# Two transformer blocks on one core: the order of work at six seams between stages

## The reference

```python
def first_block(x, c, ...):                      # two layers
    for layer in range(2):
        sh_a, sc_a, gt_a, sh_m, sc_m, gt_m = split(silu(c) @ ada_w[layer] + ada_b[layer])
        h = modulate(rms_norm(x, attn_norm[layer]), sh_a, sc_a)
        mix = diff_attention(h, ...) if layer == 0 else nsa_attention(h, ..., *shared)
        x = x + gt_a * mix
        x = x + gt_m * squared_relu_mlp(modulate(rms_norm(x, mlp_norm[layer]), sh_m, sc_m), ...)
        if layer == 0:                           # keys and values that layer 1 shares
            shared = nsa_shared_kv(modulate(rms_norm(x, kv_norm), ...), w_kv, cmp_pos, cmp_w1, cmp_w2)
    return rms_norm(x, final_norm)

def second_block(h, p, ...):                     # a gated recurrence, then dilated attention
    h = ple_add(h + mlstm_layer(h, ...), p[0], ...)
    k, v = shared_kv(h, ...)                     # k: per-head rms_norm, then rope
    h = h + dilated_layer(h, k, v, ...)          # q: per-head rms_norm, then rope
    return ple_add(h, p[1], ...)
```

## Time and profile before

| | |
|---|---|
| median of 3 runs | 1986.16 us (1981.65 to 1990.62) |
| the profiled execution's own time | 1987.13 us |
| its span, first to last instruction | 1985.3 us |
| mean granted TensorE clock | 0.995 |
| TensorE busy | 1925.7 us, 97% |
| VectorE, ScalarE, GpSimd busy | 1168.0, 855.1, 4.8 us |
| chain that ended last, by engine | TensorE 89%, VectorE 6%, ScalarE 2% |

### The profile page before, as it was taken

One profiled execution on the slowest core, in us unless ns is written; L12 is line 12 of the kernel. 1 busy time (PEld: TensorE's weight loads), 2 busy tenths in 40 slices (PEclk: granted clock), 3 DMA queues, 4 the chain that ended last, 5 costly groups with the idle time before them and its releaser, 6 DMA issues.

```text
span 1985.3 us, 24671 instructions
## 1 busy us (share of the span) xinstructions
PE 1925.7 (97%) x9444; PEld 1592.9 (80%) x9444; DVE 1168.0 (59%) x2063; ACT 855.1 (43%) x1370; POOL 4.8 (0%) x5
## 2 busy tenths in 40 slices
PE   5999999999999999999999999999999999999999
PEld 3876778888887887889888888888877888787987
DVE  7657776565657476767464343336753554766564
ACT  3246633232233543657433222234444534667453
POOL 0000000000000000000000000000000000000000
PEclk9999999999999999999899999999999999999999
DMA  9831155555544331000123232222221231241021
GB/s 358 317 150 43 49 199 209 202 184 196 199 181 148 106 108 62 1 1 1 55 85 106 85 106 86 104 92 98 85 85 64 83 136 64 85 149 64 1 96 64
DMA packets 42377, 223.87 MB, mean 113 GB/s; under 512 B 4476, under 2 KB 5244, under 8 KB 23854
## 3 DMA queue, kind: packets, MB, share of 16 engines
q1 hardware_dynamic: 41906, 222.37, 30.9%
q10 hardware_dynamic: 380, 0.28, 0.1%
HBM read 219.45 MB, written 3.19 MB: 112 GB/s over the span
## 4 chain that ended last, share of the span: by engine, by line
PE 89%; DVE 6%; ACT 2%; issue 1%; DMA 1%; SPq 0%; DVEq 0%; ACTq 0%
PE bank L434 24%; PE bank L436 24%; PE bank L435 24%; PE bank L1748 3%; PE bank L1718 2%; PE bank L3021 1%; PE bank L1707 1%; PE bank L798 1%; PE bank L2355 1%; PE bank L540 1%; PE bank L1709 1%; PE bank L818 1%; PE bank L442 1%; DMA x<-x_d 1%; PE bank L2964 1%
## 5 line engine op out<-in xcount | busy, mean ns | idle before, releaser
L434 PE MATMUL bank<-hH,wH 128*128 128x512 f32 x1280 | 501.8, 392 | 3.7 <-DVE hL L580 3.1
L436 PE MATMUL bank<-hH,wL 128*128 128x512 f32 x1280 | 498.3, 389 | 0.0
L435 PE MATMUL bank<-hL,wH 128*128 128x512 f32 x1280 | 498.1, 389 | 0.0
L1080 ACT ACTIVATE wH<-raw 128x2048 fp32r<-128x2048 f32 x64 | 122.7, 1917 | 463.1 <-PE bank L436 463.1
L1125 DVE TENSOR_TENSOR wL<-raw,wH 128x2048 fp32r<-128x2048 f32 x64 | 146.6, 2291 | 268.5 <-ACT wH L1080 268.5
L434 PEld LDWEIGHTS bank<-hH,wH 128*128 128x128 f32 x1280 | 240.3, 188 | 55.3 <-DVE hL L580 3.0
L435 PEld LDWEIGHTS bank<-hL,wH 128*128 128x128 f32 x1280 | 240.3, 188 | 50.4 <-issue 1.0
L436 PEld LDWEIGHTS bank<-hH,wL 128*128 128x128 f32 x1280 | 240.2, 188 | 50.1
L411 DVE TENSOR_TENSOR wL<-raw,wH 128x2048 fp32r<-128x2048 f32 x71 | 162.6, 2289 | 153.4 <-ACT wH L406 153.1
L406 ACT ACTIVATE wH<-raw 128x2048 fp32r<-128x2048 f32 x76 | 145.4, 1913 | 200.1 <-PE bank L436 179.1
L436 PE MATMUL bank<-aH,wL 128*128 128x512 f32 x512 | 199.2, 389 | 0.0
(11 more groups left out here) (385 smaller groups left out, 2652.1 us busy)
## 6 DMA issues: line engine op xcount, KB each, us to landing
raw<-wts_d SPq DMA_DIRECT2D x140, 1024.0 KB, 4.9
adab<-ada_d SPq DMA_DIRECT2D x72, 512.0 KB, 5.7
adac<-ada_d SPq DMA_DIRECT2D x24, 512.0 KB, 6.3
ada<-ada_d SPq DMA_DIRECT2D x3, 2048.0 KB, 27.4
bt<-bias_rows SPq DMA_DIRECT2D x1, 4096.0 KB, 16.1
ada<-ada_d SPq DMA_DIRECT2D x2, 1024.0 KB, 11.6
x<-x_d SPq DMA_DIRECT2D x1, 2048.0 KB, 12.8
peF<-ple_d SPq DMA_DIRECT2D x2, 1024.0 KB, 6.5
```

The costliest lines, as they stand in the source:

```text
L434: pe.matmul(o, l[0], r[0], start=start, stop=False)
L435: pe.matmul(o, l[0], r[1], start=False, stop=False)
L436: return pe.matmul(o, l[1], r[0], start=False, stop=stop)
L1080: act.activation(wH[:, n % 2, :], raw[:, n % 2, :], ACT.Copy).then_inc(w_hi, 1)
```

## The change

`STAT0` and the semaphore counts follow the moved work. What is left out below are declarations, counts and the removal of the GpSimd block.

First projection (`pe_first`, `dve_first`), and the same pattern for tiles 27 and 28 in `tile_mm`:

```diff
-                lo(dve, 2 * e)
                 dve.wait_ge(ada_pre, 8 * e + 8)
-                apply_dve(dve, 0, 0, ..., chunks=range(4 * e, 4 * e + 4))
+                apply_dve(dve, 0, 0, ..., chunks=range(4 * e, 4 * e + 4), first=lambda v, e=e: lo(v, 2 * e))
...
+                if n % 2 == 0:
+                    pe.wait_ge(w_hi, n + 1)
+                    for kk in range(2):
+                        pe.wait_ge(h_hi, 4 * j + kk + 1)
+                        for m in range(4):
+                            pe.matmul(bank[:, m, :], wpart(n % 2, kk, m * P, P)[0], hH[:, 4 * j + kk, :], ...)
                 pe.wait_ge(w_lo, n + 1)
-                if n == 0:
-                    first_chunk(pe, 0, lambda m: wpart(0, 0, m * P, P), 1)
-                for kk in range(1 if n == 0 else 0, 4):
+                if n % 2 == 0:
+                    for kk in range(2):            # hH x wL
...
+                    for kk in range(2):            # hL x wH
+                        pe.wait_ge(h_lo, 4 * j + kk + 1)
...
+                for kk in range(2 if n % 2 == 0 else 0, 4):
...
+            early = {27: 1, 28: 2}.get(a, 0)       # chunks whose wH products go before the wait for w_lo
+            if early:
+                order = (2, 3, 0, 1) if a == 28 else range(4)
+                pe.wait_ge(w_hi, n0 + 1)
...
```

First attention:

```diff
-                return b, (range(0, 2), range(2, 4), (), range(4, 8))[hq]
+                return b, range(2 * hq, 2 * hq + 2)
...
-        HI_AT = {4 * NT - 7: 10, 4 * NT - 4: 11, PAIRS - 7: 12, PAIRS + 2: 13}
-        LO_AT = {10: 4 * NT - 6, 11: 4 * NT - 3, 12: PAIRS - 6, 13: PAIRS + 3}
+        HI_AT = {4 * NT - 7: 10, 4 * NT - 5: 11, PAIRS - 7: 12, PAIRS + 2: 13}
+        LO_AT = {10: 4 * NT - 6, 11: 4 * NT - 4, 12: PAIRS - 6, 13: PAIRS + 3}
...
-                if v % 4 == 0 and 4 <= v < PAIRS:
-                    v_out(v // 4)
...
                 if 3 <= v < PAIRS + 3:
                     square(v - 3)
+                if v % 4 == 3 and v + 1 < PAIRS:
+                    v_out((v + 1) // 4)
...
                 for k in range(3):
-                    ada_dve(dve, 16 + 3 * n + k)
-            lo(dve, 9)
+                    if (n, k) == (7, 2):
+                        lo(dve, 9)
+                    else:
+                        ada_dve(dve, 16 + 3 * n + k)
+            def last_sum(e):                       # called behind the first maximum
+                ada_dve(e, 39)
...
```

From kv to q:

```diff
-        def pool_second(pool):                     # one GpSimd addition of 128x1984, fF for s == 1
...
+        def flat_act(act):
+            act.wait_ge(par2_in, 64)
+            act.wait_ge(half_used, N_B0)
+            for l in range(16):
+                src = bass.AP(..., offset=kv2[:, 1, 0, 2 * l:2 * l + 1].offset, ap=[..., [T, GRP], [16, NCMP]])
+                last = act.activation(fF[:, l, :]..., src, ACT.Identity, bias=sb["pos"][:, 1, l:l + 1])
+            last.then_inc(f_raw, 1)
@@ cmp_pe
             for j in range(2):
-                if j == 1:
-                    fill(pe, free, 11)
+                pe.wait_ge(w_hi, n0 + j + 1)       # fH x wH, fL x wH of eight steps
...
                 pe.wait_ge(w_lo, n0 + j + 1)       # then fH x wL
...
-            if s == 1:
-                fill(pe, free, 5)
@@ act_second
+            act.wait_ge(half_used, N_KV + 5)
+            apply_act(act, 3, lambda c: mod(48 + c), chunks=range(4))
             hi(act, N_C0 + 1)
-            apply_act(..., chunks=[0])
             hi(act, N_B0)
-            apply_act(..., chunks=[1])
             cmp_out_act(act, 0, N_B0)
-            apply_act(..., chunks=[2, 3])
+            hi(act, N_B0 + 1)
+            apply_act(..., chunks=range(4, KC))
...
-            hi(act, N_B0 + 1)
-            apply_act(..., chunks=range(4, KC))
+            flat_act(act)
             hi(act, N_C1)
+            gelu_act(act, 0)
             hi(act, N_C1 + 1)
@@ dve_second
-            apply_dve(dve, 3, 2, ..., lambda e: lo(e, N_B0 + 1), first=weights)   # weights: lo(N_C0+1), lo(N_B0)
+            apply_dve(dve, 3, 2, ..., chunks=range(4))
+            lo(dve, N_C0 + 1)
+            lo(dve, N_B0)
+            apply_dve(dve, 3, 2, ..., chunks=range(4, KC), mid=lambda e: lo(e, N_B0 + 1))
             dve.wait_ge(half_used, N_B0)
-            flat_dve(dve, 1, lambda e: lo(e, N_C1))
+            flat_dve(dve, 1)
+            gelu_dve(dve, 0, (0,))                 # steps 1 to 4
+            lo(dve, N_C1)
+            gelu_dve(dve, 0, (1,))                 # steps 5 to 7
             lo(dve, N_C1 + 1)
             lo(dve, N_B1)
-            gelu_dve(dve, 0)
-            q_lo_dve(dve, 27)
+            gelu_dve(dve, 1, (0,))
+            q_lo_dve(dve, 27, [0])
+            gelu_dve(dve, 1, (1,))
             lo(dve, N_B1 + 1)
-            gelu_dve(dve, 1)
...
+            q_lo_dve(dve, 27, [1, 2, 3])
```

The gates' transposes move from bank 7 to bank 4 and wait for fewer banks. Second attention:

```diff
-        BEGIN = [-1, FIRST[0, 0] - 6, FIRST[2, 0] - 6, FIRST[1, 0] - 6]
+        BEGIN = [1, FIRST[0, 0] - 6, FIRST[2, 0] - 6, FIRST[1, 0] - 6]
@@ nsa_pe
-            fill(pe, bank[:, 4, :], 10)
+            fill(pe, bank[:, 4, :], 4)
             for u in range(-2, UN + 5):
                 if u == BEGIN[0]:
-                    fill(pe, bank[:, 4, :], 16)
                     pe.wait_ge(acc_free[0], 4 * 15)
@@ tail(3)
-                    fill(pe, bank[:, 0, :], 9)
+                    fill(pe, bank[:, 0, :], 4)
@@ nsa_dve
+                if u == -1:
+                    q_lo_dve(dve, 28, [2, 3])      # before: all four ahead of the loop
-                if u in (0, 2, 4):
+                if u in (0, 2, 4, 6):
                     ks_dve(dve, u // 2 + 1)        # group 0 in two parts, its first ahead of the loop
+                if u == 1:
...
-                if u in (UN - 4, UN - 3):
+                if u in (UN - 1, UN):
                     dve.wait_ge(n_mm, UN - 2)
-                    lo_part(dve, HALF0["b_out"], u - (UN - 4))
+                    lo_part(dve, HALF0["b_out"], u - (UN - 1))
```

Norm before the last keys (`SUMMED`: 8 squares summed on VectorE, so one mean product instead of two) and head squares of the first two q tiles (t = 1, 2):

```diff
-        SUMMED = [7] * 9
+        SUMMED = [7] * 7 + [8, 7]
@@ head_copy
-                act.activation(hq[:, m, :], o, ACT.Square).then_inc(hn_sq, 1)
+                last = act.activation(hq[:, m, :], o, ACT.Square)
+                if t in SPLIT:                     # (1, 2)
+                    last = act.activation(sb["hqH"][:, m, :], o, ACT.Square)
+                last.then_inc(hn_sq, 1)
@@ head_pe
+                if t in SPLIT:
+                    pe.wait_ge(hn_lo, e - 4 * SPLIT[0] + 1)
+                    pe.matmul(o, sb["meanR"][:, :], sb["hqH"][:, m, :], start=True, stop=False)
+                    pe.matmul(o, sb["meanR"][:, :], sb["hqL"][:, m, :], start=False, stop=True).then_inc(hn_mm, 1)
@@ pe_fourth
-            tile_mm(pe, 64, N_DI + 2, between=lambda: head_pe(pe, 1))
-            tile_mm(pe, 65, N_DI + 4, between=lambda: head_pe(pe, 2))
+            tile_mm(pe, 64, N_DI + 2, between=lambda: head_pe(pe, 1), at=1)
+            tile_mm(pe, 65, N_DI + 4, between=lambda: head_pe(pe, 2), at=1)
```

More of the change, by code:

```diff
@@ L337, in place @@
     t("hq", [P, 4, T], "misc")
+    t("hqL", [P, 4, T], "misc", 0, F32R)
+    t("hqH", [P, 4, T], "bias", 16 * K, F32R)
     t("hr", [P, 2, T], "misc", 8 * K)
@@ L464, in tile_mm @@
             acc_wait(pe, a)
+            early = {27: 1, 28: 2}.get(a, 0)
+            if early:
+                order = (2, 3, 0, 1) if a == 28 else range(4)
+                pe.wait_ge(w_hi, n0 + 1)
+                for kk in range(early):
+                    if hbase is not None:
+                        pe.wait_ge(h_lo, hbase + kk + 1)
+                    for m in order:
+                        if kk == 0 and m == (3 if a == 27 else 1):
+                            pe.wait_ge(c_ev, a - 26)
+                        w, o = wpart(n0 % 2, kk, m * P, P), bank[:, 4 * (a % 2) + m, :]
+                        pe.matmul(o, w[0], hH[:, kk, :], start=kk == 0, stop=False)
+                        pe.matmul(o, w[0], hL[:, kk, :], start=False, stop=False)
+                pe.wait_ge(w_lo, n0 + 1)
+                for kk in range(early):
+                    for m in order:
+                        pe.matmul(bank[:, 4 * (a % 2) + m, :], wpart(n0 % 2, kk, m * P, P)[1], hH[:, kk, :],
+                                  start=False, stop=False)
             for j in halves:
@@ L478, in tile_mm @@
                     first_chunk(pe, 4 * (a % 2), lambda m: wpart(n0 % 2, 0, m * P, P), hbase + 1)
[L479 removed]
+                for kk in range(1 if ahead else early if j == 0 else 0, 4):
                     if hbase is not None:
                         pe.wait_ge(h_lo, min(hbase + 4 * j + kk + 1, KC * 9) if a == 63 else hbase + 4 * j + kk + 1)
[L482 to L485 removed]
+                    for m in range(4):
                         if (a, j, kk, m) == (29, 0, 0, 3):
@@ L507, in program @@
         sq_sum = sem("sq_sum")
-        SUMMED = [7] * 9
+        SUMMED = [7] * 7 + [8, 7]
         SUM0 = [sum(SUMMED[:s]) - s + (3 if s > 5 else 0) for s in range(9)]
```

(26 more changed lines are left out.)

178 lines of the change are left out of this document (99 added, 79 removed).

## The result

The changed kernel takes 1961.66 us (median of three runs, 1960.38 to 1964.40) against 1986.16 before: a ratio of 0.988, interval 0.9849 to 0.9910. Four further runs of it, taken later among the experiments, have the median 1964.96; over all seven it is 1963.4. The forecast was 1964.0 in a range of 1955 to 1975. The profiled execution has a span of 1959.9 us, 25.4 less than before's 1985.3, where the forecast's terms add up to 22.7. Both kernels also spread by 8 to 10 us from run to run, with the clock: at a mean granted clock of 0.997 seven runs of the kernel before take 1982.1 to 1984.0 us and four of the changed one 1961.7 to 1964.4, and at 0.993 five of before take 1988.7 to 1990.0 and one of the changed kernel 1968.3. So at an equal clock the change is worth some 20 to 21 us; the profiled pair has 0.995 before and 0.997 after.

What follows compares the result with a forecast made beforehand. TensorE, busy 97% of the span, bounds the kernel. Terms -1.0 + 4.8 + 6.0 + 3.0 + 5.5 + 4.4 = 22.7 us, from 1987.1 to 1964.4, forecast as 1964; range 1955 to 1975.

Steps and rivals of the forecast that it cites:

- the clock's part: Falls to 1.2 GHz behind idle holes: 1.6 us lost at half 5 in A, 1.2 us in C.
- A: First projection: norm products before weight subtraction; half 5's late landing leaves 0.6 us, clock fall costs 1.6: 1.0 lost.
- C: From kv projection to q: idle and fillers gone, 11.6 us, less 4.4 waiting and 1.2 clock: 6.0 won.
- the sixteen operations: ScalarE operations replacing GpSimd's one in C's chain: taken as 0.31 us each, 5.0 us, counted in full.
- the hidden fillers: Start of second attention: VectorE sets the pace, so of some 6 us of fillers and a 1.97 hole little is won.
- D: Start of second attention: fillers removed, work moved behind the first units, VectorE paces: 3.0 us won.
- B: Around first attention: row sum's wait and clock fall avoided, 2.5 us, smaller holes filled, 2.3: 4.8 won.
- The full case: Rival: clock falls nowhere and the sixteen operations are quick; 27.7 us won, 1958.5 us; chance 0.15.
- E: End of second attention: two subtractions moved, 2.12 us hole becomes about 0.9, five fillers cut, clock stays up: 5.5 won.
- F: Squares: head means as one-pass products, 3.5 us, and last norm's mean one product fewer, 0.9: 4.4 won.
- The rival in which the fillers had kept the clock up: Without fillers second attention runs at 1.2 GHz; 10 us slower after 65 us of it, 2050 if throughout; chance 0.04.

Runs made afterwards that it cites:

- the row sum's experiment: Changed kernel with the last modulation row's sum ahead of half 9's subtraction again: stretch B 601.6 us long, where other executions have 600.4 to 600.5.
- the table behind half 5: Changed kernel with the 4 MB bias table's transfer issued behind half 5 instead of ahead of it: median 1960.6 us.
- The experiments with GpSimd and the shared operations: Changed kernel with one GpSimd addition for ScalarE's sixteen operations: median 1961.7 us; with nine kept on ScalarE, seven sixteenths one VectorE addition: 1960.0.

## Why the prediction was right, and where it was not

The size was right (24.5 us between the first medians; 22 between the seven runs' 1963.4 and the 1984.8 to 1985.6 of the kernel before beside the experiments; 22.7 forecast), and each of the six stretches came within 1.5 us. That the sum came within 3 of the profiled pair is in part luck. Some steps of the working failed and made up for one another: the clock's part in A and C, the sixteen operations in C, and the hidden fillers in D.

**The clock.** The forecast took 1.6 us per fall and decided for each hole whether one comes: yes at half 5 and at C's 2.1 us, no at the others. In the profiled execution none came at half 5 or in C, and two came that no step foresaw, one at 776 behind D's new hole and one at 1465. Over all thirteen profiled executions of the changed kernel and its variants: at half 5, behind holes of 2.3 to 3.0 us, in four of the eight that had such a hole (two more had 1.0 us there, and no fall); near 735, behind the waits for wL and wH, in six of thirteen; between 1455 and 1475 in seven of thirteen. Two had one at 27 to 29 us. But for the last microseconds of the program, only at the start of the second attention did it come in all thirteen. So the right step would have been a share of 1.6 us at each hole, not a yes or no. In B that is the difference between the 2.5 us that the pair of profiles bears out and the 1.2 that the row sum's experiment gives. The kernel before has one profile, so how often its own falls come is not known; over all its 27 later runs its mean granted clock is 0.9956, over the changed kernel's seven 0.9964.

**A.** That half 5 takes back the earlier start was right in its place, mechanism and hole (2.7 forecast, 2.9 measured), and two runs show it from both sides: without the new order nothing is lost, with the table behind half 5 2.6 us more are won. The -1.6 for the clock is what was off.

**B** came 1.05 us better. The row sum and the clock were put at 2.5 us and the pair shows 2.8 (1.2 by the experiment, 1.6 for the fall that only before's profile has). The holes of the earlier trace rows were put at 2.3 us, where the traces differ by 3.0 from half 10's rounding (155.93) on; no single edit of these was undone alone, so how they share it stays open.

**C.** The chain was right in its order: load, ScalarE, fL, gelu, half C1. The sixteen operations took 6.5 us, not 5.0, 0.40 us from one to the next:

```profile
L1538 ACT ACTIVATE fF<-kv,pos 128x124 f32<-128x124 f32 x16 | 6.5, 506 | 0.0
```

The overlap of neighbours that I read from three 128x512 operations does carry over: the mean of one is 0.506 us, and the next starts 0.10 before its end. What was wrong is the length of one, for which I took the 0.395 us of a 128x128 operation. That these are 0.11 us longer may come from the strided read, but no run tries another read. The Trainium skill's estimate ("ScalarE: Activation LUTs", "Rules for kernel authors") was 6.5 us, and the trace agrees in the sum, though not in the length of one (0.40 by it, 0.51 measured). Every link behind came 0.8 to 1.0 us later than forecast (less the 5.95 us of lead: fL ended at 726.2 for 725.2, half C1's subtraction at 729.9 for 729.0). Yet the waits were 3.7 us together where 4.4 were forecast, since TensorE's own products between the first two took 3.1 us where the forecast's times leave 2.7, and the last wait, of 0.3, did not come. With no fall of the clock either, which was put at 1.2, C was 1.5 us better than forecast (these make 1.9; the 0.4 between I can't assign). No run puts C's fillers or its old order of the norm back, so the 7.5 us rest on the two traces: before 5.1 us idle and 6.5 of fillers, after 3.7 idle and no fillers. The experiments with GpSimd and the shared operations show the price of the exchange: about 1.7 us of the 3.7. The full case's C of 8.5 doesn't follow from its own terms either, which give 6.0 + 1.2 + 1.8 = 9.0.

**D** had the right size for a wrong reason. The step said that VectorE sets the pace and the 6 us of fillers hide behind it, so only about 3 are won. The fillers cost 5.8 us when put back, so this overlap was not there. The difference of 2.7 us is, as I read the rows, what the new order costs: a 1.39 us hole for q's low parts, placed between the second and third maximum, and the clock at 1.2 GHz until about 783. No run splits it. Neither engine sets the pace alone: TensorE's fillers are paid, and where TensorE gets ahead, with four fillers at the first transposes, it waits 1.92 us for VectorE.

**E.** 6.1 for 5.5; the hole became 0.68 instead of 0.9, and the clock stayed up as forecast. **F.** 4.0 for 4.4: 1.86 us per four heads instead of 1.8, against 3.43 before and not 3.60, since that is the recorded length of the group, and what follows starts before its end. TensorE never waited for the low squares.

The rival in which the fillers had kept the clock up is refuted: in none of the thirteen executions was the second attention at the lower clock for more than 7 us at a time, and the fillers themselves ran in it.

## What to carry to other kernels

An earlier start is worth what the next late transfer leaves of it: look for that transfer first, and move whatever large load stands in its queue without being needed soon. Where two engines wait for each other in turn, reordering moves the wait to the next item: two experiments each removed a hole and met one of 1.9 to 2.0 us within the next 13. And put a filler back in a run of its own before it is called hidden: 22 that looked free cost 5.8 us. And before a difference of 2 us between two profiles is explained, take a second profile of the same kernel.

## What the hardware showed beyond expectation

The clock can fall with TensorE fully busy. In the changed kernel's timeline at 1462 us TensorE has no idle time; two groups of four products from four partitions (1.98 us each) lie among full ones, and at 1465.1 a product takes 0.48 and then 0.63 us apiece until 1468.8; the first of these rows is the second group:

```profile
1462.42 1.98 PE L2315 MATMUL bank<-rows,ident 4*128 4x512 f32 x4
...
1464.90 0.40 PE L439 MATMUL bank<-wH,hL 128*128 128x512 f32 x1
1465.13 0.48 PE L437 MATMUL bank<-wH,hH 128*128 128x512 f32 x1
1465.41 0.63 PE L438 MATMUL bank<-wL,hH 128*128 128x512 f32 x1
```

The stretch from b_out's first product to the 46th rounding, which no edit touches, takes 524.4 to 524.5 us in six of the thirteen executions, 526.0 in four and 527.6 in three: steps of 1.6 us. All ten falls there, in seven executions, begin 2.1 to 3.4 us behind the start of one of these two groups. But the other six executions, and the kernel before, have the same groups and no fall. Before's profile has the short form, so 1.6 us of the pair's difference is this and not the change. That the thin products have to do with the fall is my reading of where it stands; it was not tried by itself.
